# A fused conv, attention and mixture-of-experts block on one core: start-up order of loads and products, one-piece reloads of 17 experts, and two small moves

## What is computed

```
h = rms_norm(x) * (1 + scale1) + shift1
zx, zb, zc, q_lat, kv_lat, k_rope, zg_conv, zg_mla = split(h @ w_in)
merged = sigmoid(zg_conv) * zb * conv3(zc * zx) + sigmoid(zg_mla) * attention(q_lat, kv_lat, k_rope)
x = x + gate1 * (merged @ w_o)
h2 = rms_norm(x) * (1 + scale2) + shift2
x = x + gate2 * sum over a token's 2 experts of weight * (silu(h2 @ w_gate[e]) * (h2 @ w_up[e])) @ w_down[e]
```

## Time and profile before

| | us |
|---|---|
| median of 3 runs (lowest, highest) | 509.21 (507.74, 509.48) |
| the profiled execution's own time | 509.57 |
| its span in the trace | 507.7 |
| PE busy | 479.7 (94%) |
| DVE, ACT, POOL busy | 228.4, 149.5, 153.1 |
| read from memory | 160.4 MB, 318 GB/s over the span |

### The profile page before, as it was taken

One profiled execution on the slowest core, in us unless ns is written; L12 is line 12 of the kernel. 1 busy time (PEld: TensorE's weight loads), 2 busy tenths in 40 slices (PEclk: granted clock), 3 DMA queues, 4 the chain that ended last, 5 costly groups with the idle time before them and its releaser, 6 DMA issues.

```text
span 507.7 us, 14033 instructions
## 1 busy us (share of the span) xinstructions
PE 479.7 (94%) x5759; PEld 375.6 (74%) x5760; DVE 228.4 (45%) x618; ACT 149.5 (29%) x277; POOL 153.1 (30%) x195
## 2 busy tenths in 40 slices
PE   3799999999999999999999999999999999879894
PEld 1688888888888888888888766766767667546562
DVE  1540665656564656456651444333333333232234
ACT  5022123232323231313232252433333324221240
POOL 0000010101010101010100017777777777754671
PEclk9899999999999999999999999999999999998998
DMA  8998309195979590907046999799999999999992
GB/s 346 423 437 343 171 14 409 22 412 227 409 281 396 244 391 34 407 2 307 26 167 254 383 389 408 307 384 415 427 426 428 422 425 432 426 420 425 429 398 89
DMA packets 15295, 161.90 MB, mean 319 GB/s; under 512 B 1696, under 2 KB 2976, under 8 KB 3616
## 3 DMA queue, kind: packets, MB, share of 16 engines
q1 hardware_dynamic: 15264, 161.45, 77.4%
HBM read 160.40 MB, written 1.05 MB: 318 GB/s over the span
## 4 chain that ended last, share of the span: by engine, by line
PE 78%; DMA 18%; SPq 2%; DVE 1%; issue 0%; ACT 0%; DVEq 0%; ACTq 0%
PE ps L496 74%; DMA wmix<-in_ex 7%; DMA wex<-in_ex 7%; DMA wex<-in_ada 3%; PE ps L768 1%; PE ps L805 1%; SPq L272 1%; SPq L278 1%; DVE xT L1135 1%; PE ps L769 0%; PE ps L689 0%; PE ps L690 0%; PE ps L691 0%; PE ps L676 0%; SPq L253 0%
## 5 line engine op out<-in xcount | busy, mean ns | idle before, releaser
L496 PE MATMUL ps<-act,wmix 128*128 128x256 f32 x864 | 193.5, 381 | 0.5 <-DVE act L891 0.5
L496 PEld LDWEIGHTS ps<-act,wmix 128*128 128x128 f32 x864 | 161.7, 190 | 23.5 <-issue 2.3
L377 POOL TENSOR_SCALAR work<-trig,work 128x256 f32<-128x256 f32 x70 | 64.9, 937 | 58.9 <-issue 49.6
L363 POOL TENSOR_TENSOR work<-work,trig 64x256 f32<-64x256 f32 x8 | 5.8, 719 | 240.5 <-ACT work L430 145.0
L496 PE MATMUL ps<-work 32*128 32x256 f32 (+6 forms) x864 | 72.7, 374 | 0.5 <-ACT work L490 0.5
L496 PE MATMUL ps<-wex,work 128*32 128x128 f32 (+1 forms) x1840 | 66.8, 296 | 5.3 <-DMA wex<-in_ex 4.4
L496 PEld LDWEIGHTS ps<-wex,work 128*32 128x32 f32 x1840 | 50.0, 110 | 19.3 <-issue 10.7
L496 PEld LDWEIGHTS ps<-work 32*128 32x128 f32 (+3 forms) x864 | 47.5, 168 | 13.2 <-issue 3.3
L487 ACT ACT_TABLE_LOAD x35 | 44.9, 1283 | 1.0 <-issue 0.4
L381 POOL TENSOR_TENSOR work<-work,trig 128x512 f32<-128x512 f32 x35 | 44.6, 1273 | 0.0
L1120 DVE COPY work<-ps 128x128 f32<-128x128 f32 x35 | 10.2, 291 | 74.1 <-PE ps L496 74.1
(11 more groups left out here) (191 smaller groups left out, 436.5 us busy)
## 6 DMA issues: line engine op xcount, KB each, us to landing
wex<-in_ex SPq DMA_DIRECT2D x20, 2048.0 KB, 20.9
wex<-in_ada SPq DMA_DIRECT2D x12, 2048.0 KB, 7.9
wex<-in_ex SPq DMA_DIRECT2D x20, 1024.0 KB, 22.2
wmix<-in_ex SPq DMA_DIRECT2D x8, 2048.0 KB, 20.4
wmix<-in_mix_even SPq DMA_DIRECT2D x4, 3200.0 KB, 15.7
wmix<-in_mix_odd SPq DMA_DIRECT2D x4, 3008.0 KB, 14.6
work<-in_ex SPq DMA_DIRECT2D x8, 1024.0 KB, 21.6
wmix<-in_ex SPq DMA_DIRECT2D x8, 1024.0 KB, 21.0
```

The source lines that it names most:

```text
L363: nc.gpsimd.tensor_tensor(k_sq[0:ROPE, :], k_sq[0:ROPE, :], k_rope_sq[0:ROPE, :], ALU.add).then_inc(sq_joined, 1)
L377: nc.gpsimd.tensor_scalar(comb_both[:, rows], slot_row[:, rows], lane_now, None, ALU.is_equal).then_inc(comb_half, 1)
L496: return nc.tensor.matmul(out, lhsT, rhs, start=start, stop=stop, **kw)
```

## The change

- `small` is loaded in two parts: its first 105 columns at once, the router's bias and weights behind the first head's weights, with a semaphore of their own (`router_landed`). `const` is loaded in two parts too: `ident` early, the rest behind the second latent load.
- The first latent load goes ahead of the second `w_ada` block; the later order is otherwise kept.
- `latent` now takes one slice k and a range of tiles, and the slices are woven between the `w_ada` blocks. `warm(18)` and `warm(4)` put products of ones, whose results are not used, ahead of the sum of squares and ahead of the first block.
- Experts 0 to 2, the fifth and sixth place, and the reloads for e = 7 to 23 (experts 14 to 30) are loaded whole: one transfer of 3 MB in rows of 24 KB, or 1 MB and 2 MB in the seventh place. SP raises `down_landed` itself. A whole reload waits for `down_ready` alone. The reloads for e = 0 to 6 and for e = 24 stay split.
- Expert 3's gate and up are asked for at `ada_summed` 8 instead of `ada_turned` 12.
- The three rank products go ahead of two of the four clearing products.

```
             def ring(n, src):
...
             ada_load(0)
-            sp.dma_start(const[:], const_d).then_inc(const_landed, 16)
+            sp.dma_start(ident, const_d[:, 0:P]).then_inc(ident_landed, 16)
+            lat_load(0)
             ada_load(1)
-            lat_load(0)
+            lat_load(1)
+            sp.dma_start(const[:, P:], const_d[:, P:]).then_inc(const_landed, 16)
             sp.dma_start(posi, pos_d).then_inc(pos_landed, 16)
-            lat_load(1)
             ada_load(2)
             ada_load(3)
             lat_load(2)
             lat_load(3)
             mix_load(0)
+            sp.dma_start(small[:, SMALL_FIRST:], small_d[:, SMALL_FIRST:]).then_inc(router_landed, 16)
...
+            def whole_load(s, e):
+
+                if s < len(ex_place):
+                    sp.dma_start(ex_place[s], ex_d[e]).then_inc(gu_landed[s], 16)
+                    sp.sem_inc(down_landed[s], 16)
+                else:
+                    head_load(s, e)
+                    tail_load(s, e)
...
+            sp.wait_ge(ada_summed, HEADS)
+            gu_load(OWN - 1, OWN - 1)
             sp.wait_ge(ada_turned, 4 + HEADS)
-            expert_load(OWN - 1, OWN - 1)
+            down_load(OWN - 1, OWN - 1)
...
                 upto = windows_before(sp, e + 1)
-                sp.wait_ge(gu_ready, upto)
-                gu_load(s, e + EX_SLOTS)
-                sp.wait_ge(down_ready, upto)
-                down_load(s, e + EX_SLOTS)
+                if e < EX_SLOTS or e + EX_SLOTS == EXPERTS - 1:
+                    sp.wait_ge(gu_ready, upto)
+                    gu_load(s, e + EX_SLOTS)
+                    sp.wait_ge(down_ready, upto)
+                    down_load(s, e + EX_SLOTS)
+                else:
+                    sp.wait_ge(down_ready, upto)
+                    whole_load(s, e + EX_SLOTS)
...
             pe.wait_ge(setup_done, 4)
+            warm(18)
...
+            warm(4)
             pe.wait_ge(c_ready, 1)
             ada_first(0)
             ada_turn(0)
+            latent(0)
             ada_first(1)
+            latent(1, range(0, 3))
             ada_turn(1)
-            latent(0)
-            latent(1)
+            latent(1, range(3, LAT_TILES_ALL))
+            latent(2)
             ada_first(2)
+            latent(3, range(0, 3))
+            ada_turn(2)
+            latent(3, range(3, LAT_TILES_ALL))
             ada_first(3)
-            ada_turn(2)
+            latent(4)
             ada_turn(3)
-            latent(2)
-            latent(3).then_inc(lat_ready, 1)
+            for k in range(5, KT):
+                last = latent(k)
+            last.then_inc(lat_ready, 1)
...
             pe.wait_ge(y_cleared, 1)
-            for b in (1, 3):
-                mm(ps[:, 4 + b, :], ones[:], ycomb, True, True)
             pe.wait_ge(onehot_ready, 1)
             mm(ps[:, 1, 0:64], before, oh[:, 2].rearrange("p t n -> p (t n)"), True, False, skip_group_check=True)
...
+            for b in (1, 3):
+                mm(ps[:, 4 + b, :], ones[:], ycomb, True, True)
```

More of the change, by code:

```diff
@@ L49 @@
 SMALL, N_SMALL = places(SMALL_WIDTHS)
+SMALL_FIRST = SMALL["b_router"][0]
 CONST, N_CONST = places(CONST_WIDTHS)
@@ L198, in block_kernel @@
         x_landed, small_landed, const_landed, pos_landed = sem("x_landed"), sem("small_landed"), sem("const_landed"), sem("pos_landed")
+        ident_landed, router_landed = sem("ident_landed"), sem("router_landed")
         mix_landed = [sem("mix_landed0"), sem("mix_landed1")]
@@ L257, in _ @@
             sp.dma_start(xT[:], xT_d).then_inc(x_landed, 16)
-            sp.dma_start(small[:], small_d).then_inc(small_landed, 16)
+            sp.dma_start(small[:, 0:SMALL_FIRST], small_d[:, 0:SMALL_FIRST]).then_inc(small_landed, 16)
             def ada_load(n):
                 sp.dma_start(wex[:, n, 0:ADA_COLS], ada_d[n]).then_inc(ada_landed[n], 16)
[L264 to L268, removed]
             def gu_load(s, e):
@@ L273, in gu_load, with tail_load, head_load @@
                 else:
-                    gu_head_load(e)
-                    gu_tail_load(e)
+                    sp.dma_start(split_head, ex_d[e][:, 0:GU_COLS // 2]).then_inc(gu_landed[s], 16)
+                    sp.dma_start(split_tail[:, 0:GU_COLS // 2], ex_d[e][:, GU_COLS // 2:GU_COLS]).then_inc(gu_landed[s], 16)
             def down_load(s, e):
                 sp.dma_start(place_down(s), ex_d[e][:, GU_COLS:]).then_inc(down_landed[s], 16)
-            def expert_load(s, e):
-                gu_load(s, e)
-                down_load(s, e)
+            def tail_load(s, e):
+                sp.dma_start(split_tail, ex_d[e][:, GU_COLS // 2:]).then_inc(gu_landed[s], 16)
+                sp.sem_inc(down_landed[s], 16)
+            def head_load(s, e):
+                sp.dma_start(split_head, ex_d[e][:, 0:GU_COLS // 2]).then_inc(gu_landed[s], 16)
+            def whole_load(s, e):
+                if s < len(ex_place):
+                    sp.dma_start(ex_place[s], ex_d[e]).then_inc(gu_landed[s], 16)
+                    sp.sem_inc(down_landed[s], 16)
+                else:
+                    head_load(s, e)
+                    tail_load(s, e)
             def ring(n, src):
@@ L326, in _ @@
                 if 1 <= c < OWN:
-                    expert_load(c - 1, c - 1)
+                    whole_load(c - 1, c - 1)
+            sp.wait_ge(ada_summed, HEADS)
+            gu_load(OWN - 1, OWN - 1)
             sp.wait_ge(ada_turned, 4 + HEADS)
-            expert_load(OWN - 1, OWN - 1)
+            down_load(OWN - 1, OWN - 1)
             last = EX_SLOTS - 1
             sp.wait_ge(merged_ready, HEADS)
-            gu_tail_load(last)
-            down_load(last, last)
+            tail_load(last, last)
             for n in range(2):
                 sp.wait_ge(wo_ready, 2 * n + 2)
-                expert_load(OWN + n, OWN + n)
+                whole_load(OWN + n, OWN + n)
             sp.wait_ge(h2r_ready, 2)
             sp.wait_ge(lg_ready, 1)
-            gu_head_load(last)
+            head_load(last, last)
             sp.wait_ge(table_ready, 1)
@@ L518, in ada_turn @@
                 if n == 0:
-                    pe.wait_ge(const_landed, 16)
+                    pe.wait_ge(ident_landed, 16)
                 if n >= 2:
@@ L522, in ada_turn, with latent, warm @@
                 nc.tensor.transpose(ps[:, (6, 7)[n % 2], 0:P], merged[:, n, 0:P], ident).then_inc(ada_turned, 1)
-            def latent(n):
+            def latent(k, tiles=range(LAT_TILES_ALL)):
+                n = k // 2
                 pe.wait_ge(lat_landed[n], 16)
                 w = ring_slot[0][:, n * LAT_PART:(n + 1) * LAT_PART].rearrange("p (k m c) -> p k m c", k=2, m=LAT_TILES_ALL)
[L528 to L531, removed]
-                return last
+                pe.wait_ge(h_ready, k + 1)
+                for m in tiles:
+                    last = mm(lat_ps[m], w[:, k % 2, m, :], hT[:, k, :], k == 0 and m % 2 == 0, k == KT - 1, skip_group_check=True)
+                return last
+            def warm(count):
+                for i in range(count):
+                    mm(ps[:, 7, 0:P], ones[:], ones[:], True, True)
             pe.wait_ge(setup_done, 4)
+            warm(18)
             for k in range(KT):
@@ L570, in _ @@
             last.then_inc(lat_ss_ready, 1)
+            pe.wait_ge(const_landed, 16)
             pe.wait_ge(krope_ready, 1)
@@ L677, in _ @@
                 if h == 5:
+                    pe.wait_ge(router_landed, 16)
                     for k in range(KT):
@@ L1017, in _ @@
                 if h == 5:
+                    dve.wait_ge(router_landed, 16)
                     dve.wait_ge(part_ready, 1)
```

## The result

The changed kernel is slower by a small, resolved amount. Its median is 509.92 us (20 runs, 508.91 to 512.37), that of the kernel before, run beside it, 508.27 us (20 runs, 507.25 to 509.69). The ratio is 1.003 with a 95% interval of 1.0021 to 1.004: +1.65 us where -1.35 us was forecast. The time lies inside the range, the sign is wrong, and by the 0.5% bound it counts as no change.

The account below looks back on a forecast made before the run. PE was taken to set the pace to 290 us, with PE and DMA strands almost level at the end. Start -2.4, whole reloads +0.8 and rank +0.25 gave -1.35, 509.21 to 507.9 us; 8-in-10 range 505.8 to 510.4.

Parts of the forecast that it names:

- the 0.5% bound: Whole kernel: a measurement tells about 0.5%, 2.5 us, from no change; below 506.7 is faster, above 511.8 slower.
- that of the warm products: Start, before 25 us: the two `warm` calls win and cost nothing, covered by PE's wait for block 2.
- the 2 us wait: Start: PE, done with slices 1 and 2 near 25 us, waits 2 us for block 2, landing at 27.0.
- the first part: What bounds the kernel: from 60 to 290 us PE sets the pace, so the start's saving is carried through unchanged.
- the 2.2 us forecast for the request that starts the stream: Expert stage: expert 3's replacement is asked for about 2.2 us sooner than 329.81 us.
- Start: Latent products woven between `w_ada` blocks: `lat_ready` lets the first head's next load go at 44.7 instead of 47.1 us, -2.4 us.
- Rank: Ahead of the first gather: PE waits 0.9 us for the one-hot table, reaching the first selection later; +0.25 us.
- Whole reloads: Expert 28 waits for down too, 2.5 us; long rows save 1.05, old slack takes 0.64: +0.8 us.
- Expert 3: 2 MB moved from 269 to about 262 us; costed at nothing, since the stream runs dry at 328 us anyway.
- B: Expert stage: joined transfers save 0.15 us or more per expert, rank move gives its full -0.56; 505.9 us. Chance 0.25.
- C: Start: PE's clock falls in the wait for block 2, costing 1.7 us; sum +0.05, 509.3 us. Chance 0.18.
- D: Whole reloads hold expert 28 back and long rows run slower beside PE; 511.9 us at 0.2 us per expert. Chance 0.12.

Follow-up runs that it names:

- the one measured beside the others: Changed kernel with a loop bound on PE set by a maximum with 0 instead of a move, and one instruction more ahead: 510.26 us, ratio 1.0026.
- 43 small ones: Changed kernel with 43 products of one column by 32 rows (172 instructions) in place of the warm products: 507.19 us, ratio to before 0.9974.
- 64: Changed kernel with 64 products of one column by 32 rows (256 instructions) in place of the warm products: 508.02 us, ratio to before 1.0.
- 22 small products: Changed kernel with 22 products of one column by 32 rows (88 instructions) in place of the warm products: 510.53 us, ratio to before 1.0038.

## Why the prediction was wrong

**The step that failed** is that of the warm products. It said: "So PE's own speed before 25 us is worth nothing, the two `warm` calls included: what they win on block 0 is covered by the 2 us wait, and so is what they could cost by running into the squares". As a sentence on work and waits it held: `lat_ready` is at 44.67 us with and without them. But it priced the calls as PE time only. They are also 88 instructions ahead of everything else that PE runs, and they move the entry of the expert loop to where its code is not at hand, and the branch there takes 3.25 us in place of 0.32: a stop of 2.23 us in the changed kernel, 2.83 us in the one measured beside the others, and 3.06 us on the median. With it fell a sentence of the first part, "there PE sets the pace, and whatever the start saves is carried through unchanged". It is carried to 294.8 us and lost at 298 us; of the 2.2 us forecast for the request that starts the stream, 0.83 us are left. None of my rivals had it.

**The rest of the sum, without the warm products,** was -1.35 us; that kernel gave 507.2 us with a ratio of 0.9972, -1.1 us by the median beside it (508.3) and -1.4 by the ratio.

- Start: -2.4 forecast, -2.52 us at `lat_ready`. The landings of blocks 2 and 3 were right to 0.1 us. Wrong was block 1's (18.96, not 17.7 us), so the cover behind it was 0.53 us and not 2 us. That did no harm, but the sentences that leaned on a 2 us cover leaned on less than they said.
- Rank: +0.25 forecast; 0.4 us at the gather in the traces, nothing resolved at the end.
- Whole reloads: +0.8 forecast; 0.6 us in the medians, whose intervals overlap. Expert 28 is 1.23 us later behind the stream's start, for 1.45 forecast, and the rate is 430 for 426 GB/s, near the 431 GB/s that I took from the first head's load.
- Expert 3: nothing forecast, nothing found.

**The rivals.** B, a faster stream, asked for 0.15 us or more for each expert; the rate rose by 0.9%, 0.07 us for 7.4. C, a fall of the clock in the wait for block 2, was not there: the block took 1.95 us, and the granted clock is 1.00 on both sides of it. It is no answer to +1.65 us either, though its 509.3 us is the nearest number on my list. D, a slower stream, is contradicted by the 430 GB/s. The time fell into the range for a reason that was not among those that made the range.

**What stays open.** Why the packet moves when it does, and what fills the 2.4 to 2.6 us between its move and the end of the branch. And why the small stops, 0.2 to 0.8 us, are at 310 us in one kernel, 312 in another, 343 in a third: they too move with the number of instructions. They lie at packets as well: PE goes on 2.2 to 2.6 us behind a packet of its code (packet at 309.8 us and PE at 312.11 in the kernel before, 307.6 and 309.94 without warm products, 339.9 and 342.47 with 43 small ones, 340.5 and 343.03 with 64). But not every packet brings a stop, and which ones do was not worked out. That the median of the change lies 0.4 us above its profiled run may come from a longer stop in other executions; this was only argued. What the record shows is that the runs of one kernel with the stop lie far apart, 509.28 to 513.06 us with 22 small products, and that the four slowest of these have a mean granted clock of 0.989 to 0.994, the four fastest of 0.996 to 0.997.

A second thing varies from execution to execution: the clock behind the waits of the last experts. In the kernel without warm products expert 28's block took 3.54 us in the profiled execution, in the changed kernel 1.96 us. With whole reloads nothing behind expert 28 waits for DMA, so such a block lengthens the run; none of the prediction's terms or of the differences above takes it into account.

## What to carry to other kernels

An added instruction that does no work can have a price even where its engine is idle: on an engine with a loop behind a long straight stretch, it shifts where the loop's entry falls in the packets of code. Here 88 instructions cost 3 us and 172 nothing. When a change adds or takes away instructions, look in the chain of waits for "issue", ask the source view of the loop's line how long its branch took, and the DMA view of that moment for the queue of instructions. Where they agree, add or remove padding until the packet moves while the engine is at work. And price each part of a change by a kernel without that part: here the moved rank products and the whole reloads together cost about 1 us by the medians, the warm products 3, and what was left was worth twice the whole forecast.

## What the runs showed of the hardware

- PE stood still for 2.1 to 4.4 us at the entry of a loop with all its semaphores up, 2.8 to 3.0 us counted from the packet with its code; the branch itself took 3.1 to 5.4 us, against 0.32 us in the eight kernels without the stop. 88 instructions of 14131, some 290 us earlier, decide whether it does.
- With 256 PE instructions more, the packets of PE's code lie where they lay without them (258.7, 285.9 and 299.8 us for 259.1, 285.5 and 299.8): one packet is 256 instructions.
- In the changed kernel seven packets of PE's code came between 300.5 and 350 us, in the loop's first round, and none between 350 and 476.5 us, when its other rounds ran: PE kept the loop's code, some 7 x 16 = 112 KB.
- The clock behind such a stop can be either level: after 2.23 and 2.83 us of idle time the block ran at full clock (1.96 and 1.95 us), after 4.41 us at 0.51. But the length of the pause does not settle it. Two kernels started expert 28 after the same 1.78 us of waiting for its load: the changed one in 1.96 us (granted clock 1.00), the one without warm products in 3.54 us (0.52). The Trainium skill, "TensorE: Matmul & The Clock Gate", section "HAM oscillation", has a wait between bursts restart the engine throttled when it is long enough; the block after the 4.41 us agrees, and the two equal waits of 1.78 us show that here the wait alone does not tell which it will be.
- Transfers of 3 MB in rows of 24 KB ran at 430 GB/s beside PE, loads of 1 and 2 MB back to back at 426: joining them saves about 0.07 us for an expert.
